# Three groups of TensorE transposes read their tiles as fp32r instead of fp32

## The chip, the cores and the metric

One core of one Trainium2 chip. The metric is the device time of one execution in microseconds (us). TensorE appears in the profile as PE (matmuls) and PEld (weight loads), VectorE as DVE, ScalarE as ACT, GpSimd as POOL, and the queue that starts most of the DMAs as SP.

## The reference

One layer with 1024 positions of width 1024: a root-mean-square norm with a scale and shift computed from c, one input projection, 8 stick-breaking heads and 8 forgetting heads of width 64, a gate, an output projection, and a last norm. Cut to what matters here:

```python
h = rmsnorm(x, g_norm) * (1.0 + scale) + shift          # scale, shift, gate from silu(c) @ w_ada + b_ada
z = h @ w_in                                            # q, k, v of both kinds, gate path, forget logits
# stick-breaking heads: a[t,s] = sigmoid(z_ts) * prod_(s<j<t) (1 - sigmoid(z_tj)), s < t
# forgetting heads:     p = softmax(q k^T * scale + cum_q - cum_k), s <= t
o = probabilities @ v                                   # for each head
y = concat([rmsnorm(o_sb, g), rmsnorm(o_fx, g)]) * silu(g_path)
x = x + (1.0 + gate) * (y @ w_out)
return rmsnorm(x, g_final)
```

## The kernel before

All large products take each operand as a sum of two fp32r halves (hi and lo; fp32r is a 4-byte number with fewer mantissa bits) and add three products: hi with hi, lo with hi, hi with lo. The heads are worked in 8 pairs. A pair has 16 units: two heads by eight blocks of 128 queries. Pairs alternate between stick-breaking (even) and forgetting (odd). Unit g has n = g % 8 + 1 blocks of 128 keys.

The order on each engine is written out by hand. For unit g TensorE runs, in this order:

- half of a projection unit (lines 1581, 1582 and 1589: 16 matmuls of 512 columns in two halves), or in the last pair a part of the output product (line 1680);
- at i = 14 and i = 2 of a pair (i = g % 16) the four transposes of half of a pair's v (`transpose_v`, line 1633), 16 such runs;
- the scores of unit g + 2 (lines 1612 and 1613; a bf16 matmul, line 1616, adds the mask);
- for even g the products of probabilities and v of the two units before (line 1668, the moving operand is 256 or 128 columns);
- the transposes of unit g's probabilities (`transpose_probs`, line 1644), one for each 128x128 block, so n of them in a row.

The scores of a stick-breaking unit go through ACT (two sigmoids, lines 909 and 910), DVE (a scan, line 1237) and POOL (a product, line 698) into the tile U, which is a part of `work`. Those of a forgetting unit go through DVE (line 1250), ACT (exp, line 914), DVE (a reciprocal, line 1260) and POOL (line 704). Then TensorE transposes U into one of two PSUM banks, up to four blocks to a bank. ACT copies the bank as pt_hi (line 949) and DVE subtracts this from the bank as pt_lo (line 1298). These two are what line 1668 reads. `next_bank` (line 1623) waits until DVE is done with the item two before.

Before the pairs, the first 512 rows of x are transposed in eight runs of four (`turn_x`, line 1486), each between projection matmuls. TensorE's first work is a product that spreads c over the partitions (line 1723); ACT (line 782) and DVE (line 1136) wait for it.

The tile `work` has 9 rows of 1024 per partition: U is rows 0 and 1, VT (v before its transpose) is row 6, the first four blocks of x are rows 0 to 3. `ident` is a 128x128 fp32 identity that is loaded from memory. In `nc.tensor.transpose(out, in_, identity)` the block is the stationary operand (the one that PEld loads) and the identity is the moving one.

Of the kernel before, what the change touches and what calls it, by code (L numbers as in the profile page):

```python
# [25 lines left out]
def hybrid_trunk_kernel(nc, x, x_t, c, w_ada_t, const_cols, w_blocks, w_f, w_out, g_final, identity, out):  # L26
    fp32 = mybir.dt.float32
    fp32r = mybir.dt.float32r
# [4 lines left out]
    P = 128  # L33
    SEQ, D = x.shape
# [27 lines left out]
    def tgroups(g):  # L62

        n = g % TB + 1
        return [(a, min(a + 4, n)) for a in range(0, n, 4)]
# [103 lines left out]
    with ctx:  # L169
        def sb(name, shape, dt=fp32):  # L170
            return ctx.enter_context(nc.sbuf_tensor(name, shape, dt))

        def sem(name):
            return ctx.enter_context(nc.semaphore(name))
# [16 lines left out]
        def sb_with_early(name, shape, early_shapes):  # L191

            base = (nc.sbuf_base + 31) // 32 * 32
            whole = sb(name, shape, fp32r)
            size = 4
            for n in shape[1:]:
                size *= n
            assert nc.sbuf_base == base + size
            early, at = [], base
            for i, early_shape in enumerate(early_shapes):  # L200
                early.append(nc.alloc_sbuf_tensor_at(f"{name}_early{i}", early_shape, fp32, offset=at))
                at += 4 * int(np.prod(early_shape[1:]))
            assert at <= nc.sbuf_base
            return whole, early

        h_lo = sb("h_lo", [P, DC, SEQ], fp32r)


        stacks, (w_early, ada_early, x_row6, _, x_row7) = sb_with_early(
            "stacks", [P, 2, 2, 3, SEQ], [[P, 2, DC, P], [P, 3, SEQ], [P, SEQ], [P, 4, SEQ], [P, SEQ]])  # L210
        v_stack, (x_late,) = sb_with_early("v_stack", [P, 2, 2, TB, P], [[P, DC, HALF]])

        pt_hi, (squares_junk, root_diag, roots) = sb_with_early("pt_hi", [P, TB, 2 * P],
                                                                [[P, SEQ], [P, HALF], [P, HALF]])
        pt_lo, (x_rows_late,) = sb_with_early("pt_lo", [P, TB, 2 * P], [[P, 2, SEQ]])
        work = sb("work", [P, 9, SEQ])
        U = [work[:, 0, :], work[:, 1, :]]
        R = [work[:, 2, :], work[:, 3, :]]
        CUM = [work[:, 4, :], work[:, 5, :]]
        VT = work[:, 6, :]  # L220
# [6 lines left out]
        gate_half = spare[:, 0, :]  # L227
        o_shift = spare[:, 1, :].rearrange("p (s n) -> p s n", s=2)
        ident = sb("ident", [P, P])
        ident_bf = sb("ident_bf", [P, P], bf16)  # L230
        mask_f = sb("mask_f", [P, 2, P])
        mask_bf = sb("mask_bf", [P, 2, P], bf16)
# [57 lines left out]
        s_ones = sem("s_ones")  # L290
# [50 lines left out]
        s_id = sem("s_id")  # L341
# [21 lines left out]
        X_BANK = TRANS[0]  # L363
# [3 lines left out]
        def x_row(t):  # L367

            return (work[:, t, :] if t < 4 else (x_rows_late[:, 0, :], x_rows_late[:, 1, :], x_row6[:], x_row7[:])[t - 4])
# [35 lines left out]
        Z = [G_T, R[0], R[1], VT, CUM[0], G_T, R[0], R[1]]  # L405
        RES = Z[STORED:] + [U[1], O_T, U[0]]
        SQUARES = U[0]

# [209 lines left out]
        def _(pool):  # L618
# [75 lines left out]
            def sb_probs(g):  # L694

                n = (g % TB + 1) * P
                pool.wait_ge(s_scan, SB_UNIT[g])
                nc.gpsimd.tensor_tensor(U[g % 2][:, 0:n - 1], U[g % 2][:, 0:n - 1], R[g % 2][:, 1:n],  # L698
                                        ALU.mult).then_inc(s_prob, 1)

            def fx_probs(g):
                n = (g % TB + 1) * P
                pool.wait_ge(s_inv, FX_UNIT[g])
                nc.gpsimd.tensor_scalar(U[g % 2][:, 0:n], U[g % 2][:, 0:n], row_inv[:, g % 2:g % 2 + 1], 1.0,  # L704
                                        ALU.mult, ALU.mult).then_inc(s_prob, 1)
# [71 lines left out]
        def _(act):  # L777
# [121 lines left out]
            def scores_out(g):  # L899
                for j, (a, e) in enumerate(pieces(g)):  # L900
                    if is_sb(g):
# [6 lines left out]
                        bank = SCORE[(S_PIECE[g, j] - 1) % 3][:, 0:e - a]  # L908
                        nc.scalar.activation(U[g % 2][:, a:e], bank, ACT.Sigmoid)
                        nc.scalar.activation(R[g % 2][:, a:e], bank, ACT.Sigmoid, scale=-1.0).then_inc(s_sig, 1)  # L910
                if not is_sb(g):
                    n = (g % TB + 1) * P
                    act.wait_ge(s_max, FX_UNIT[g])
                    nc.scalar.activation(U[g % 2][:, 0:n], U[g % 2][:, 0:n], ACT.Exp, bias=neg_max[:, g % 2:g % 2 + 1],  # L914
                                         accum_out=row_sum[:, g % 2:g % 2 + 1]).then_inc(s_exp, 1)
# [175 lines left out]
        def _(dve):  # L1091
# [37 lines left out]
            nc.vector.memset(ones_square[:], 1.0).then_inc(s_ones, 1)  # L1129
            nc.vector.memset(ss_o, 0.0).then_inc(s_ones, 1)  # L1130
            dve.wait_ge(s_id, 16)
            nc.vector.tensor_copy(ident_bf[:], ident[:]).then_inc(s_maskb, 1)
            dve.wait_ge(s_mask, 3)
            nc.vector.tensor_copy(mask_bf[:], mask_f[:]).then_inc(s_maskb, 1)
# [338 lines left out]

        @block.tensor
        def _(pe):
            pe.wait_ge(s_id, 16)

            def turn_x(n):

                d = first_pieces[n][1]  # L1480
                pe.wait_ge(s_xna, 1 + (d >= 2) + (d >= 4))
                pe.wait_ge(s_xnd, 1 + (d >= 2) + (d >= 4))
                if n >= 1:
                    pe.wait_ge(s_hfull, n)
                for t in range(4):
                    last = nc.tensor.transpose(X_BANK[:, t * P:(t + 1) * P],
                                               x_row(t)[:, d * P:(d + 1) * P], ident[:])
                last.then_inc(s_xt, 1)

            def spread_roots():  # L1490
# [38 lines left out]
            def first_piece(n):  # L1529
# [26 lines left out]
                if n + 1 < DC:  # L1556
                    turn_x(n + 1)
# [62 lines left out]
            def next_bank(item):  # L1620
                n = T_ITEM[item]
                if n > 2:
                    pe.wait_ge(s_tfree, n - 2)
                return TRANS[(n - 1) % 2]

            def transpose_v(p, j):

                pe.wait_ge(s_phi, unit_no[p, "v", j] + 1)
                if (p, j) == (0, 0):
                    pe.wait_ge(s_plo, LO_UNITS[-1, "f", 1])  # L1630
                bank = next_bank(("V", p, j))
                for k in range(4):
                    last = nc.tensor.transpose(bank[:, k * P:(k + 1) * P],
                                               VT[:, (4 * j + k) * P:(4 * j + k + 1) * P], ident[:])
                last.then_inc(s_t, 1)

            def transpose_probs(g):
                pe.wait_ge(s_prob, g + 1)
                if g == 0:
                    pe.wait_ge(s_hfull, DC)  # L1640
                for j, (a, e) in enumerate(tgroups(g)):
                    bank = next_bank(("T", g, j))
                    for k in range(a, e):
                        last = nc.tensor.transpose(bank[:, (k - a) * P:(k - a + 1) * P],  # L1644
                                                   U[g % 2][:, k * P:(k + 1) * P], ident[:])
                    last.then_inc(s_t, 1)

            def sum_squares(p):
# [73 lines left out]
            for half in range(NHALF):  # L1722
                last = nc.tensor.matmul(psum[:, half, :], ones_square[0:1, :], CUM[0][0:1, half * HALF:(half + 1) * HALF],
                                        start=True, stop=True)
            last.then_inc(s_call, 1)
            turn_x(0)
            for n in range(2 * DC):
                if n == 2 * DC - 2:
# [80 lines left out]
```

## Time and profile before

| | |
|---|---|
| time, median of 3 runs | 741.24 us (740.69 to 743.7) |
| the profiled execution | 742.23 us, of which its span is 740.4 us |
| PE busy | 703.8 us, 95% |
| PEld busy | 587.7 us, 79% |
| DVE, ACT, POOL busy | 482.9, 426.0, 370.6 us |
| chain that ended last | PE 80%, DVE 9%, ACT 6% |
| mean granted TensorE clock | 0.988 |

A matmul's row lasts from its start to its modelled end, and rows of PE overlap: the next one starts while the last drains. So how long a matmul holds the engine is read from the distance between starts and not from its duration. A merged row (x8) lasts from the first start to the last end; that length less one duration, over the number less one, is the distance.

### The profile page before, as it was taken

Reading aid. Unit: us, or ns where it says so; the run is one execution under the profiler, and the core shown is the slowest. Engines: PE = TensorE matmul, PEld = TensorE weight load, DVE = VectorE, ACT = ScalarE, POOL = GpSimd, SP = SyncE. Lnnn points to the kernel's source line nnn. Section 1 sums busy time; section 2 is a strip of 40 time slices with the busy share of each in tenths; the row PEclk is TensorE's granted clock in tenths of the full one; section 3 lists DMA queues with packets and bytes.
Section 4 is the critical chain, followed back from the end, with each engine's and each line's share of the span. In section 5 each row is a group of like instructions: output and inputs, shape, how many; then the busy total and the mean of one; then the engine's idle time right before and its main releaser. Section 6 shows DMA issues by size and latency. Waiting matters only on the chain.

```text
span 740.4 us, 10802 instructions
## 1 busy us (share of the span) xinstructions
PE 703.8 (95%) x3830; PEld 587.7 (79%) x3830; DVE 482.9 (65%) x992; ACT 426.0 (58%) x885; POOL 370.6 (50%) x329
## 2 busy tenths in 40 slices
PE   2989988999999999999999999999999999999995
PEld 0667877888888888888888888888888878888884
DVE  4977998646655776465558664765586654555566
ACT  5875767555675656466757565666565665323222
POOL 1020465567885455688756555866575643321100
PEclk9999999999999999999999999999999997999998
DMA  9942231223442110334430102455312095882222
GB/s 350 409 155 86 74 126 32 86 100 114 143 147 102 38 58 0 100 114 153 161 103 12 58 23 87 145 172 168 102 45 79 22 361 165 255 284 86 86 114 114
DMA packets 35463, 93.14 MB, mean 126 GB/s; under 512 B 4297, under 2 KB 5961, under 8 KB 34898
## 3 DMA queue, kind: packets, MB, share of 16 engines
q1 hardware_dynamic: 28450, 73.71, 28.8%
q0 software_dynamic: 5376, 14.68, 6.2%
q10 hardware_dynamic: 1584, 4.05, 1.4%
q8 instruction: 31, 0.51, 0.3%
q14 instruction: 22, 0.18, 0.1%
HBM read 68.81 MB, written 23.63 MB: 125 GB/s over the span
## 4 chain that ended last, share of the span: by engine, by line
PE 80%; DVE 9%; ACT 6%; issue 3%; POOL 1%; DMA 0%; DVEq 0%; ACTq 0%; POOLq 0%
PE psum L1680 12%; PE psum L1581 12%; PE psum L1582 12%; PE psum L1589 12%; PE psum L1668 8%; PE psum L1644 8%; PE psum L1613 4%; PE psum L1612 4%; DVE stacks L1205 2%; DVE work L1237 2%; PE psum L1511 1%; PE psum L1616 1%; ACT work L910 1%; DVE pt_lo L1298 1%; ACT pt_hi L949 1%
## 5 line engine op out<-in xcount | busy, mean ns | idle before, releaser
L1581 PE MATMUL psum<-h_hi,w_hi 128*128 128x512 f32 x448 | 186.2, 416 | 1.9 <-DVE stacks L1205 1.9
L1582 PE MATMUL psum<-h_lo,w_hi 128*128 128x512 f32 x448 | 176.6, 394 | 0.0
L698 POOL TENSOR_TENSOR work<-work 128x127 f32<-128x127 f32 (+3 forms) x64 | 82.9, 1295 | 155.4 <-DVE work L1237 155.4
L949 ACT ACTIVATE pt_hi<-psum 128x512 fp32r<-128x512 f32 (+1 forms) x192 | 87.7, 490 | 103.4 <-PE psum L1644 100.3
L1298 DVE TENSOR_TENSOR pt_lo<-psum,pt_hi 128x512 fp32r<-128x512 f32 (+1 forms) x192 | 100.9, 552 | 59.6 <-ACT pt_hi L949 57.3
L1237 DVE TENSOR_TENSOR_SCAN work<-work 128x128 f32<-128x128 f32 (+3 forms) x64 | 96.2, 1504 | 38.7 <-ACT work L910 38.4
L1589 PE MATMUL psum<-h_hi,w_lo 128*128 128x512 f32 x448 | 120.2, 390 | 0.0
L1581 PEld LDWEIGHTS psum<-h_hi,w_hi 128*128 128x128 f32 x448 | 85.2, 190 | 17.4 <-issue 2.7
L1589 PEld LDWEIGHTS psum<-h_hi,w_lo 128*128 128x128 f32 x448 | 84.2, 188 | 18.6
L1582 PEld LDWEIGHTS psum<-h_lo,w_hi 128*128 128x128 f32 x448 | 85.1, 190 | 14.9
L704 POOL TENSOR_SCALAR work<-work,small 128x128 f32<-128x128 f32 (+3 forms) x64 | 47.8, 747 | 92.4 <-DVE small L1260 92.2
L1644 PE MATMUL psum<-ident,work 128*128 128x128 f32 x576 | 87.8, 279 | 2.4 <-DVE pt_lo L1298 1.5
L914 ACT ACTIVATE work<-work,small 128x128 f32<-128x128 f32 (+3 forms) x64 | 49.8, 778 | 61.3 <-DVE small L1255 61.0
L1668 PE MATMUL psum<-pt_hi,v_stack 128*128 128x256 f32 x320 | 80.4, 286 | 2.0 <-DVE pt_lo L1298 2.0
L1668 PE MATMUL psum<-pt_lo,v_stack 128*128 128x256 f32 x320 | 75.0, 281 | 0.0
L923 ACT ACTIVATE spare<-psum 64x256 f32<-64x256 f32 x64 | 24.3, 380 | 77.6 <-PE psum L1668 77.2
L1612 PE MATMUL psum<-stacks 128*128 128x512 f32 (+1 forms) x192 | 65.7, 342 | 1.9 <-DVE small L1250 1.9
L1644 PEld LDWEIGHTS psum<-ident,work 128*128 128x128 f32 x576 | 62.2, 142 | 4.5 <-issue 1.6
L1613 PE MATMUL psum<-stacks 128*128 128x512 f32 (+1 forms) x192 | 63.6, 344 | 0.0
L1668 PEld LDWEIGHTS psum<-pt_hi,v_stack 128*128 128x128 f32 x320 | 61.3, 192 | 2.2 <-DVE pt_lo L1298 2.2
L1668 PEld LDWEIGHTS psum<-pt_lo,v_stack 128*128 128x128 f32 x320 | 61.0, 191 | 0.1
L1269 DVE TENSOR_TENSOR work<-psum,spare 64x256 f32<-64x256 f32 x64 | 26.7, 416 | 51.0 <-ACT spare L923 50.7
(186 smaller groups left out, 1349.5 us busy)
## 6 DMA issues: line engine op xcount, KB each, us to landing
w_raw<-in_w_blocks SPq DMA_DIRECT2D x30, 512.0 KB, 4.3
w_split_scratch<-work SPq DMA_DIRECT2D x16, 512.0 KB, 3.3
work<-in_x SPq DMA_DIRECT2D x12, 512.0 KB, 7.7
work<-in_w_ada_t SPq DMA_DIRECT2D x10, 512.0 KB, 7.7
y_split_scratch<-work SPq DMA_DIRECT2D x10, 512.0 KB, 3.3
v_stack_early<-in_w_ada_t SPq DMA_DIRECT2D x8, 512.0 KB, 3.2
work<-forget_scratch SPq DMA_DIRECT2D x8, 512.0 KB, 5.3
work<-in_w_out SPq DMA_DIRECT2D x16, 256.0 KB, 3.4
```

What stands on the lines that cost most here:

```text
L698: nc.gpsimd.tensor_tensor(U[g % 2][:, 0:n - 1], U[g % 2][:, 0:n - 1], R[g % 2][:, 1:n], ALU.mult).then_inc(s_prob, 1)
L949: nc.scalar.activation(pt_hi[:, a:e, (g % 2) * P:(g % 2 + 1) * P], bank, ACT.Copy).then_inc(s_thi, 1)
L1237: nc.vector.tensor_tensor_scan(R[g % 2][:, 0:n][:, ::-1], R[g % 2][:, 0:n][:, ::-1], R[g % 2][:, 0:n][:, ::-1], 1.0, ALU.mult, ALU.bypass) ...
L1298: nc.vector.tensor_tensor(pt_lo[:, a:e, q0:q0 + P], bank, pt_hi[:, a:e, q0:q0 + P].bitcast(fp32), ALU.subtract).then_inc(s_tfree, 1)
L1581: nc.tensor.matmul(bank, hi, h_hi[:, c_, cols], start=(c_ == 0), stop=False)
L1582: nc.tensor.matmul(bank, hi, h_lo[:, c_, cols], start=False, stop=False)
L1589: last = nc.tensor.matmul(bank, lo, h_hi[:, c_, cols], start=False, stop=(c_ == DC - 1))
L1612: nc.tensor.matmul(bank[:, 0:c1 - c0], q, stacks[:, p % 2, a, 1, c0:c1], start=True, stop=False)
L1613: last = nc.tensor.matmul(bank[:, 0:c1 - c0], q, stacks[:, p % 2, a, 2, c0:c1], start=False, stop=not diagonal)
L1644: last = nc.tensor.transpose(bank[:, (k - a) * P:(k - a + 1) * P], U[g % 2][:, k * P:(k + 1) * P], ident[:])
L1668: last = nc.tensor.matmul(OUT[:, c0:2 * P], v_stack[:, p % 2, a, k, :], src[:, k, c0:2 * P], start=(k == 0 and n == 0), stop=(k == qb + 1 ...
L1680: last = nc.tensor.matmul(psum[:, bank, :], y_, w_[:, m, cols], start=(j == 0 and k == 0), stop=(j == PAIRS // 2 - 1 and k == 2))
```

## The change

It gives the memory of `work` a second name, `turned`, of type fp32r, makes an fp32r copy of the identity on DVE, and transposes probabilities, v and x with both operands and the output named as fp32r. It is the same memory, the same words, the same instructions in the same order. TensorE's first wait, for the load of the identity, becomes a wait for the copy.

```diff
--- before.py
+++ after.py
@@ -213,7 +213,10 @@
         pt_hi, (squares_junk, root_diag, roots) = sb_with_early("pt_hi", [P, TB, 2 * P],
                                                                 [[P, SEQ], [P, HALF], [P, HALF]])
         pt_lo, (x_rows_late,) = sb_with_early("pt_lo", [P, TB, 2 * P], [[P, 2, SEQ]])
+        work_at = (nc.sbuf_base + 31) // 32 * 32
         work = sb("work", [P, 9, SEQ])
+
+        turned = nc.alloc_sbuf_tensor_at("turned", [P, 9, SEQ], fp32r, offset=work_at)
         U = [work[:, 0, :], work[:, 1, :]]
         R = [work[:, 2, :], work[:, 3, :]]
         CUM = [work[:, 4, :], work[:, 5, :]]
@@ -227,6 +230,7 @@
         gate_half = spare[:, 0, :]
         o_shift = spare[:, 1, :].rearrange("p (s n) -> p s n", s=2)
         ident = sb("ident", [P, P])
+        ident_r = sb("ident_r", [P, P], fp32r)
         ident_bf = sb("ident_bf", [P, P], bf16)
         mask_f = sb("mask_f", [P, 2, P])
         mask_bf = sb("mask_bf", [P, 2, P], bf16)
@@ -1129,6 +1133,7 @@
             nc.vector.memset(ones_square[:], 1.0).then_inc(s_ones, 1)
             nc.vector.memset(ss_o, 0.0).then_inc(s_ones, 1)
             dve.wait_ge(s_id, 16)
+            nc.vector.tensor_copy(ident_r[:], ident[:]).then_inc(s_ones, 1)
             nc.vector.tensor_copy(ident_bf[:], ident[:]).then_inc(s_maskb, 1)
             dve.wait_ge(s_mask, 3)
             nc.vector.tensor_copy(mask_bf[:], mask_f[:]).then_inc(s_maskb, 1)
@@ -1473,7 +1478,7 @@
 
         @block.tensor
         def _(pe):
-            pe.wait_ge(s_id, 16)
+            pe.wait_ge(s_ones, 3)
 
             def turn_x(n):
 
@@ -1483,8 +1488,8 @@
                 if n >= 1:
                     pe.wait_ge(s_hfull, n)
                 for t in range(4):
-                    last = nc.tensor.transpose(X_BANK[:, t * P:(t + 1) * P],
-                                               x_row(t)[:, d * P:(d + 1) * P], ident[:])
+                    last = nc.tensor.transpose(X_BANK[:, t * P:(t + 1) * P].bitcast(fp32r),
+                                               turned[:, t, d * P:(d + 1) * P], ident_r[:])
                 last.then_inc(s_xt, 1)
 
             def spread_roots():
@@ -1630,8 +1635,8 @@
                     pe.wait_ge(s_plo, LO_UNITS[-1, "f", 1])
                 bank = next_bank(("V", p, j))
                 for k in range(4):
-                    last = nc.tensor.transpose(bank[:, k * P:(k + 1) * P],
-                                               VT[:, (4 * j + k) * P:(4 * j + k + 1) * P], ident[:])
+                    last = nc.tensor.transpose(bank[:, k * P:(k + 1) * P].bitcast(fp32r),
+                                               turned[:, 6, (4 * j + k) * P:(4 * j + k + 1) * P], ident_r[:])
                 last.then_inc(s_t, 1)
 
             def transpose_probs(g):
@@ -1641,8 +1646,8 @@
                 for j, (a, e) in enumerate(tgroups(g)):
                     bank = next_bank(("T", g, j))
                     for k in range(a, e):
-                        last = nc.tensor.transpose(bank[:, (k - a) * P:(k - a + 1) * P],
-                                                   U[g % 2][:, k * P:(k + 1) * P], ident[:])
+                        last = nc.tensor.transpose(bank[:, (k - a) * P:(k - a + 1) * P].bitcast(fp32r),
+                                                   turned[:, g % 2, k * P:(k + 1) * P], ident_r[:])
                     last.then_inc(s_t, 1)
 
             def sum_squares(p):
```

## Rows read from the trace of the kernel before

**Rows 1.** The page: busy us, share of the span, instructions of each engine.
```profile
PE 703.8 (95%) x3830; PEld 587.7 (79%) x3830; DVE 482.9 (65%) x992; ACT 426.0 (58%) x885; POOL 370.6 (50%) x329
```

**Rows 2.** Waits of PE, 135 to 600 us: total, times, longest, all in us.
```profile
PE psum L1633 <- ACT work L886: 1.7, 4, 0.4
PE psum L1581 <- DVE stacks L1205: 1.0, 3, 0.5
PE psum L1644 <- DVE v_stack L1277: 0.6, 3, 0.2
```

**Rows 3.** Groups by line and form, PE matmuls: count, busy us, mean ns.
```profile
L1644 PE MATMUL psum<-ident,work 128*128 128x128 f32 x576 | 87.8, 279 | 2.4 <-DVE pt_lo L1298 1.5 <-DVE v_stack L1277 0.6 <-POOL work L698 0.2
L1668 PE MATMUL psum<-pt_hi,v_stack 128*128 128x128 f32 x64 | 14.3, 223 | 0.0
```

**Rows 4.** The same view, weight loads.
```profile
L1644 PEld LDWEIGHTS psum<-ident,work 128*128 128x128 f32 x576 | 62.2, 142 | 4.5 <-issue 1.6 <-DVE v_stack L1277 1.3 <-POOL work L698 1.2
L1668 PEld LDWEIGHTS psum<-pt_hi,v_stack 128*128 128x128 f32 x320 | 61.3, 192 | 2.2 <-DVE pt_lo L1298 2.2
L1653 PEld LDWEIGHTS psum<-ones,work 128*128 128x128 f32 x16 | 1.9, 191 | 0.2 <-POOL work L773 0.2
```

**Rows 5.** Timeline at 306.6 us, unit 49: start, length, engine, line.
```profile
306.65 0.20 PEld L1644 LDWEIGHTS psum<-ident,work 128*128 128x128 f32 x2
306.70 0.39 PE L1644 MATMUL psum<-ident,work 128*128 128x128 f32 x2
...
306.82 0.19 PEld L1581 LDWEIGHTS psum<-h_hi,w_hi 128*128 128x128 f32 x1
...
306.85 0.48 PE L1581 MATMUL psum<-h_hi,w_hi 128*128 128x512 f32 x1
```

**Rows 6.** Timeline, a run of eight transposes in unit 55.
```profile
333.42 1.04 PE L1644 MATMUL psum<-ident,work 128*128 128x128 f32 x8
```

**Rows 7.** Timeline: fp32 matmuls of 512 columns, then loads before one-column fp32 matmuls.
```profile
47.34 1.02 PE L1494 MATMUL psum<-pt_hi_early,ones 128*128 128x512 f32 x2
...
694.70 1.86 PEld L1653 LDWEIGHTS psum<-ones,work 128*128 128x128 f32 x16 [0.19 <-POOL work L773]
```

**Rows 8.** Timeline, four places where TensorE waits for others.
```profile
220.19 0.55 PE L1644 MATMUL psum<-ident,work 128*128 128x128 f32 x3 [0.21 <-DVE v_stack L1277]
...
261.10 0.47 PE L1581 MATMUL psum<-h_hi,w_hi 128*128 128x512 f32 x1 [0.31 <-DVE stacks L1205]
...
291.00 0.66 PE L1633 MATMUL psum<-ident,work 128*128 128x128 f32 x4 [0.43 <-ACT work L886]
...
297.27 0.86 PEld L1644 LDWEIGHTS psum<-ident,work 128*128 128x128 f32 x8 [0.17 <-POOL work L698]
```

**Rows 9.** Chain that ended last, three of its pieces: start, us, what.
```profile
114.62 7.16 issue
...
253.79 0.50 ACT work L910
...
696.64 35.55 PE psum L1680 x156
```

**Rows 10.** Timeline: the first DVE copy and TensorE's first matmul.
```profile
2.69 0.23 DVE L1132 CAST ident_bf<-ident 128x128 bf16<-128x128 f32 x1 [1.66 <-DMA ident<-in_identity]
...
2.71 1.22 PE L1723 MATMUL psum<-work,ones 1*128 1x512 f32 x1 [2.71 <-DMA ident<-in_identity]
```

**Rows 11.** Timeline at 125 us: a wait, and matmuls after it.
```profile
124.98 0.39 PE L1668 MATMUL psum<-pt_hi,v_stack 128*128 128x256 f32 x1 [2.03 <-DVE pt_lo L1298]
...
128.15 0.63 PE L1582 MATMUL psum<-h_lo,w_hi 128*128 128x512 f32 x1
128.58 0.63 PE L1581 MATMUL psum<-h_hi,w_hi 128*128 128x512 f32 x1
```

**Rows 12.** Timeline: POOL's product of unit 35 and the transposes' loads behind it.
```profile
240.03 1.10 POOL L698 TENSOR_TENSOR work<-work 128x511 f32<-128x511 f32 x1
...
241.44 0.42 PEld L1644 LDWEIGHTS psum<-ident,work 128*128 128x128 f32 x4
```

## The prediction

> **What bounds the kernel now.** I read the page first: PE is busy for 703.8 of 740.4 us, while no other compute engine reaches two thirds [rows 1]; by its part on the chain, PE holds 80% of what ended last. A PE row overstates the engine's time, so I went on to what PE waits for. Between 135 and 600 us all its idle time is some 3 us [rows 2]. So in the loop over the pairs TensorE's own stream is the clock, and a nanosecond taken out of it counts, unless the next wait takes it back. The chain by time shows three exceptions, where it runs over ACT, DVE and POOL: the second half of x's projections, units 6 to 10 (with 7.16 us that the profile doesn't explain [rows 9]), and units 113 to 115 with table loads on ACT.
>
> **How long a transpose holds TensorE.** Eight in a row last 1.04 us [rows 6]; less the 0.273 us that one lasts, over 7, that is 0.109 us from start to start. What is it made of? Two things could set it. *The moving side:* a plain fp32 matmul of 512 columns starts 0.43 us after the last (1.02 less 0.59) [rows 7], 0.83 ns a column, so 128 columns would take 0.107 us. Fp32r matmuls of 512 columns take 0.23 us each (156 in 35.55 us) [rows 9], half of it, and an fp32r matmul of 128 columns lasts 223 ns, where the transpose lasts 279 [rows 3]: 56 ns more, which is one more pass of 128 columns. *The load:* the two loads of unit 49 last 0.20 us together, one alone 0.142, so the second started 0.06 us after the first, and the first matmul started 0.05 us after its load [rows 5]. The load of a transposed block is thus through in about 0.06 us and lies beside a stream of 0.107. All other 4-byte loads, fp32 (line 1653) and fp32r (line 1668), last 191 ns against 142 [rows 4], and loads with almost nothing between them follow each other after 0.111 us (1.86 less 0.19, over 15) [rows 7]. So for a plain load the name fp32 or fp32r makes no difference, and being a transpose makes it 50 ns shorter.
>
> **The change, part by part.**
>
> 1. *Transposes.* As fp32r the identity should stream in one pass, 0.056 us. Then the load of the next block is what is late: 0.06 us. No row shows an fp32r transpose. The bounds: 0.056 us if the load hides after all, 0.111 us if the load becomes that of an ordinary fp32r weight. I take 0.065, near the load step of rows 5 and a little above it, because the step was read at 10 ns. That is 0.044 us less for each.
>
> 2. *The last transpose of each run gains nothing.* The matmul behind it needs an ordinary load. In unit 49 line 1581 is loaded at 306.82, its row begins at 306.85 but lasts 0.48 instead of 0.39, so it really streams from about 306.93, 0.11 us after its load began [rows 5]. That load may begin only when the last transpose has begun, so 0.11 us pass in either kernel. Runs: 128 of probabilities, 16 of v, 8 of x. Transposes: 576 [rows 3], 64 and 32, by the loops. Steps that gain: 448 + 48 + 24 = 520. At 0.044 us: 22.9 us.
>
> 3. *What the waits take back.* Where TensorE arrives early at a wait, what was saved since the start of that wait's chain is lost. There is one of each kind in [rows 8].
>    - Line 1581 waits for DVE in unit 40, at 261.10. Its chain left TensorE before ACT's row at 253.79 [rows 9], and units 38 and 39 lie in between, 6 + 7 steps, 0.57 us. It recurs in three pairs: 1.7 us.
>    - v's transposes wait for ACT (291.00, four times). The chain starts at the first bank of unit 45, three steps: 0.5 us in all.
>    - Unit 47 waits for POOL (297.27, four times). In between are the transposes of v and of unit 46, 3 + 6 steps, 0.4 us each: 1.6 us.
>    - The second bank of units 14, 30, 46 and so on waits for v_stack (220.19, seven times, slight in four). Three steps: 0.9 us.
>    - Off the chain: units 6 to 10, 16 steps, 0.7 us; the last run of x, and units 113 to 115 with v: 9 steps, 0.4 us.
>    Sum 5.8 us. Elsewhere POOL is done with the probabilities well before TensorE wants them. One of the closest covers is unit 35's: POOL ends at 241.13 and the transposes' first load begins at 241.44 [rows 12], 0.31 us later, and between its scores and there lie 1 + 3 + 2 steps, 0.26 us. So hardly anything new becomes late. If that cover were gone, all 22.9 us would be lost and not more.
>
> 4. *The copy of the identity.* It stands on DVE ahead of ident_bf. The cast there takes 0.23 us, and TensorE's first matmul, which starts with the identity's landing at 2.71 [rows 10], now waits for the copy. ACT and DVE wait for that product, and their chain leads to the first transpose of x. It costs 0.25 us; below, nothing, if the loads of x turn out to be later. ident_bf and the mask copies behind it have 65 us of room.
>
> 5. *The second name* costs no instruction. What ACT, DVE and POOL do has the same words and forms as before.
>
> Sum: 22.9 - 5.8 - 0.25 = 16.8 us. The profiled execution took 742.23 us, so it would take 725.4. The median of the runs shown is 1.0 us below it, 741.24, which makes 724.4; I say 725.0.
>
> **Two rules beside the rows.** The rows say that a transposed block's load is through in 0.06 us [rows 5]. The Trainium skill (TensorE: Matmul & The Clock Gate, LDWEIGHTS) gives a load as the number of columns over 1.2, that is 107 ns for 128, at any type without fast loading. By that rule the load alone would keep the step where it is and the change would bring nothing. The trace agrees with it for plain loads and not for those of transposes. The Trainium skill (same page, Terms) calls the transpose mode four times faster for fp32. The trace shows a factor of two in the stream (0.107 us against two passes of 0.107 for a plain fp32 product), which leaves one more factor of two for the type; if the fp32 transposes had all four already, nothing would be left.
>
> **The rivals.**
>
> - *A: as worked out.* 718 to 732 us. The low end has a step of 0.056: 520 x 0.053 = 27.6, less 4 for waits, 718. The high end has a load that is only partly hidden, a step of 0.083, half way between 0.056 and 0.111: 520 x 0.026 = 13.5, less 3.5, 732. Chance 0.74.
> - *B: the step does not fall.* Either a transpose named fp32r is loaded as ordinary weights are, every 0.111 us, or a 4-byte word goes through the array in two passes whatever its name. For it: the 191 ns of all fp32r loads [rows 4]. Against it: fp32 and fp32r loads are alike there, so the type is not what makes the transposes' loads short. 520 x 0.002 = 1.0 us, and the copy: 741 to 743 us. Chance 0.19. This is also the case in which the change doesn't do what it says.
> - *C: slower, by the clock.* After the wait of 2.03 us at 124.98 the granted clock fell to half (1.2 GHz) and 512 columns took 0.43 us instead of 0.23 from 126 to 129 us [rows 11]; that cost 1.8 us. If the waits of step 3, each longer by up to 0.6 us, made the clock fall too, 18 of them would cost 32 us less the 16.8 saved: 757 us. Slower by more than 3.7 us begins at 12 such falls. Against it: the waits of [rows 8] are 0.2 to 0.43 us long and the clock stayed at full speed, and with 0.6 more they are still half of that 2.03. Chance 0.06. The Trainium skill (TensorE: Matmul & The Clock Gate, PE-mode transpose) has it that transposes do not count as work for the clock; here eight in a row run at full speed [rows 6]. By that rule shorter transposes would, if anything, help.
> - Faster than 718: 0.01.
>
> **How the numbers follow.** The likeliest is A. A's own range leaves out 0.26, so the range reaches up over B: 718 to 742.5. A measurement of this kernel can tell about 0.5% from no change, 3.7 us. Faster than 737.5: A, 0.75. Within: B, 0.19. Slower than 745: C, 0.06.
>
> **What would show it.** A right: the matmuls of lines 1644, 1633 and 1486 last some 55 ns less, 220 to 225 instead of 273 to 279; their loads still last about 142; eight in a row last 0.65 to 0.72 us instead of 1.04; line 1581 behind them still lasts 0.48; and the idle time between 135 and 600 us [rows 2] grows by 4 to 5 us. If the loads of line 1644 last 190, it is B by the load; if the matmuls still last 273, it is B by the stream. Windows with a low clock where the kernel before has none would be C. The copy is seen by TensorE's first start, 2.95 instead of 2.71. I would be wrong in size if the steps fell as said and the gaps at [rows 8] grew by more than the savings between; then more of the chain hangs on ACT, DVE and POOL than I counted.

## The result, and the profile after

The kernel after takes 738.85 us (median; 737.14 to 740.58), the kernel before 742.45 on the same chips (740.24 to 744.02). The ratio is 0.9949, with an interval of 0.994 to 0.9959. So it is faster by 3.8 us, where 16.8 were forecast: the direction held, the size did not.

The profiled execution of after took 739.11 us, its span is 737.3 and its mean granted clock 0.984, where before had 742.23, 740.4 and 0.988. In after the lines shift by 5: 1644 is 1649, 1633 is 1638, 1486 is 1491, 1581 is 1586, 1668 is 1673, and the ACT, DVE and POOL lines by 4 or 5. The page of after, engines' busy us and shares, against [rows 1]:

```profile
PE 696.8 (95%) x3830; PEld 580.5 (79%) x3830; DVE 483.6 (66%) x993; ACT 425.8 (58%) x885; POOL 371.1 (50%) x329
```

The groups by line and form of after, PE and then loads, against [rows 3, 4]: count, busy us, mean ns, idle time before.

```profile
L1649 PE MATMUL psum<-ident_r,turned 128*128 128x128 f32 x576 | 72.7, 253 | 6.1 <-POOL work L702 2.5 <-DVE pt_lo L1303 1.8 <-DVE v_stack L1282 0.9
...
L1649 PEld LDWEIGHTS psum<-ident_r,turned 128*128 128x128 f32 x576 | 57.4, 142 | 8.3 <-POOL work L702 3.7 <-DVE v_stack L1282 2.5 <-issue 1.9
```

The load's row is unchanged at 142 ns. The matmul's fell from 279 to 253 and not to 220, so the load that looks the same no longer keeps up. The distance shows it. Timeline of after, unit 49 and then the run of eight of unit 55, against [rows 5, 6]: start, length.

```profile
307.00 0.23 PEld L1649 LDWEIGHTS psum<-ident_r,turned 128*128 128x128 f32 x2
307.18 0.19 PEld L1586 LDWEIGHTS psum<-h_hi,w_hi 128*128 128x128 f32 x1
...
333.33 0.86 PE L1649 MATMUL psum<-ident_r,turned 128*128 128x128 f32 x8
334.02 0.46 PE L1586 MATMUL psum<-h_hi,w_hi 128*128 128x512 f32 x1
```

Eight in a row last 0.86 us: less one duration of 0.25, over 7, that is 0.087 us a step. The loads of unit 49 say the same (0.23 less 0.142), where [rows 5] had 0.06. Read singly, in before each load begins 2 ns after the transpose ahead of it and the next transpose 107 ns later: the stream was the limit. In after the loads follow each other every 83 to 88 ns, and a transpose starts some 36 ns after its load. It is so throughout: in the runs of two and more blocks the second load begins 62 ns after the first in before and 86 in after (medians of the 112 runs of probabilities).

Waits of PE from 135 to 600 us in after, against [rows 2]: total, times, longest.

```profile
PE psum L1586 <- DVE stacks L1210: 2.0, 3, 0.9
PE psum L1638 <- ACT work L890: 1.6, 4, 0.4
PE psum L1649 <- DVE v_stack L1282: 0.9, 3, 0.4
PE psum L1649 <- POOL work L702: 0.3, 1, 0.3
```

They grew by 1.5 us in all. At two of the places of [rows 8], timeline of after:

```profile
221.18 0.45 PE L1649 MATMUL psum<-ident_r,turned 128*128 128x128 f32 x3 [0.39 <-DVE v_stack L1282]
...
261.70 0.47 PE L1586 MATMUL psum<-h_hi,w_hi 128*128 128x512 f32 x1 [0.72 <-DVE stacks L1210]
```

Both came later than in [rows 8] (220.19 and 261.10), though TensorE had saved time on the way. Something had been lost earlier. Timeline of after between 108 and 133 us, all the places where PE waits:

```profile
108.02 0.91 PE L1649 MATMUL psum<-ident_r,turned 128*128 128x128 f32 x8 [1.75 <-DVE pt_lo L1303]
109.91 0.77 PE L1586 MATMUL psum<-h_hi,w_hi 128*128 128x512 f32 x1 [0.99 <-DVE stacks L1210]
...
131.66 0.54 PE L1649 MATMUL psum<-ident_r,turned 128*128 128x128 f32 x4 [2.29 <-POOL work L702]
```

From the second on, and again behind the third, the granted clock is at half. The view by windows (us in the window, busy us and instructions of each engine, then PEclk), first of before and then of after:

```profile
108.00:112.00 4.00, 2.51 (x14) 2.09 (x15) 3.92 (x7) 2.66 (x6) 3.31 (x3) 1.00 0.57 183
125.00:129.00 4.00, 4.00 (x14) 3.32 (x15) 3.94 (x5) 2.19 (x6) 3.92 (x4) 0.58 0.17 9
133.00:137.00 4.00, 4.00 (x27) 3.49 (x26) 2.75 (x4) 1.98 (x7) 1.03 (x1) 1.00 0.39 61
```

```profile
108.00:112.00 4.00, 3.00 (x13) 2.51 (x14) 3.89 (x8) 3.39 (x8) 2.93 (x3) 0.61 0.74 246
125.00:129.00 4.00, 4.00 (x23) 3.41 (x23) 3.73 (x5) 2.19 (x6) 3.92 (x3) 1.00 0.17 9
133.00:137.00 4.00, 4.00 (x12) 3.09 (x12) 2.96 (x3) 1.85 (x5) 0.77 (x1) 0.60 0.57 102
```

The last column but two is the clock. Before has one fall here, behind the wait at 124.98 [rows 11]; after has two, at 109 and 133. In the last window after gets through 12 matmuls where before gets through 27; part of that is another mix, since before has come to the short ones of unit 12 there. Like for like, a projection product takes 0.43 us at half clock and 0.23 at full. How far ahead or behind after is, by the start of a unit's transposes (worked out from the trace, after less before):

```
unit   start in before   after   again (experiment 1)
  6        103.20        -0.84        -0.70
 12        136.34        +1.93        -0.69
 48        303.27        +0.34        -2.26
114        604.39        -2.58        -4.83
127        683.47        -3.16        -3.89
```

The profiled execution of after loses 2.8 us between units 6 and 12. From 12 to 114 it gains 4.5 us.

### The profile page after: what moved, and what is told of

The parts are those of the page before. It is cut to its first block, busy times and chain, and to the rows that moved or that the text cites. A ratio compares the mean times of both kernels' runs of the same rounds, so it can differ in the third digit from the quotient of the medians.

```text
span 737.3 us, 10803 instructions
## 1 busy us (share of the span) xinstructions
PE 696.8 (95%) x3830; PEld 580.5 (79%) x3830; DVE 483.6 (66%) x993; ACT 425.8 (58%) x885; POOL 371.1 (50%) x329
## 4 chain that ended last, share of the span: by engine, by line
PE 63%; DVE 13%; ACT 9%; POOL 7%; issue 7%; DMA 0%; DVEq 0%; ACTq 0%; POOLq 0%
PE psum L1685 11%; PE psum L1586 11%; PE psum L1587 10%; PE psum L1594 10%; PE psum L1673 7%; PE psum L1649 4%; POOL work L702 3%; PE psum L1618 3%; PE psum L1617 3%; DVE work L1242 3%; POOL w_lo L648 2%; DVE stacks L1210 2%; DVE work L1255 2%; DVE pt_lo L1303 1%; ACT work L918 1%
## 5 line engine op out<-in xcount | busy, mean ns | idle before, releaser
L1594 PE MATMUL psum<-h_hi,w_lo 128*128 128x512 f32 x448 | 121.9, 394 | 0.0
L1649 PE MATMUL psum<-ident_r,turned 128*128 128x128 f32 x576 | 72.7, 253 | 6.1 <-POOL work L702 2.5
L1649 PEld LDWEIGHTS psum<-ident_r,turned 128*128 128x128 f32 x576 | 57.4, 142 | 8.3 <-POOL work L702 3.7
```

What stands on the lines that cost most here:

```text
L1594: last = nc.tensor.matmul(bank, lo, h_hi[:, c_, cols], start=False, stop=(c_ == DC - 1))
```

## The theories

Three things can have made 3.8 of 16.8, and the experiments are to size each. The step: a transposed block is loaded more slowly when it is named fp32r, although its row looks the same, so a step saves 0.022 us and not 0.044. The waits: they take back more than the quarter that I counted. The clock: falls that before doesn't have, or has where they are hidden. The main rivals are that the limit in the step is not the load (but the matmul itself, a write, or a fixed 86 ns for each fp32r instruction), and that the clock's falls follow the waits and not anything else.

## Experiments

**1. The same kernel again.** Nothing is edited.

> The changed kernel itself, once more, as the yardstick beside the three others on the same chip. Theory (a run of n transposes costs 308 + 109 n ns in fp32 and about 345 + 86 n ns in fp32r; two falls of the TensorE clock between 105 and 140 us cost what was gained there): 0.995 of the kernel before, mean granted clock 0.983 to 0.988, and the executions with the higher clock are the shorter ones. Rival (the saving is the same in every execution, and the clock has no part in it): no relation of clock and time.

739.15 us (738.32 to 739.46), ratio 0.996 (0.9948 to 0.9972). Its profiled execution had a mean clock of 0.986 and none of the falls at 109 and 133. It had the one of before instead. Its timeline, PE:

```profile
110.06 0.47 PE L1586 MATMUL psum<-h_hi,w_hi 128*128 128x512 f32 x1 [0.99 <-DVE stacks L1210]
110.36 0.40 PE L1587 MATMUL psum<-h_lo,w_hi 128*128 128x512 f32 x1
...
124.36 0.39 PE L1673 MATMUL psum<-pt_hi,v_stack 128*128 128x256 f32 x1 [1.86 <-DVE pt_lo L1303]
...
126.21 0.63 PE L1587 MATMUL psum<-h_lo,w_hi 128*128 128x512 f32 x1
```

The same two waits stand ahead of 110.06, and the clock stayed. It lost nothing to unit 12 and was 4.8 us ahead at unit 114 (table above). So the falls at 109 and 133 belong to an execution and not to the kernel. In its five executions the one with the highest clock is the shortest (738.32 at 0.986) and those at 0.983 and 0.984 take 739.15 to 739.46, as expected. But this execution met another: behind a wait of 1.73 us it ran the last pair's products at half clock from 606.8 us on, some 4 us earlier than in after, and its lead fell from 4.8 to 2.9 us at unit 116. All executions with a trace have a fall near there, before's too; from 606 to 630 us the granted clock is 0.79 in before and after and 0.72 here.

**2. fp32r only from pair 1 on.** x, v of pair 0 and units 0 to 15 stay fp32.

```diff
-                    last = nc.tensor.transpose(X_BANK[:, t * P:(t + 1) * P].bitcast(fp32r), ...)
+                    last = nc.tensor.transpose(X_BANK[:, t * P:(t + 1) * P], x_row(t)[:, d * P:(d + 1) * P], ident[:])
...
+                    if p >= 1:
...
+                        if g >= STEPS:
```

> x, v of the first pair and the probabilities of units 0 to 15 are transposed as fp32 again, the rest stays fp32r. Theory (what was gained before unit 12 is given back between 105 and 140 us, by falls of the clock that the kernel before does not have on its critical path): the first 140 us are those of the kernel before, clock 0.988, one fall at about 125 us; the gain behind it is 4.7 us, so about 0.9937 of the kernel before, 1 us faster than the changed kernel. Rival (early transposes gain as the later ones do): the 1.4 us of the early runs are lost, about 0.997 of the kernel before, 1.4 us slower than the changed kernel.

738.65 us (737.18 to 740.58), ratio 0.9956 (0.994 to 0.9972). The time lies between the two expectations and settles nothing: it scatters over 3.4 us, and with the clock (0.989 took 737.18, 0.984 took 739.94 and 740.58). The profile is clearer. Its fall is at 124.8, as in before, and behind it unit 114 begins 4.4 us ahead of before, unit 127 5.0. That is what fp32r in pairs 1 to 7 was worth in this execution, the shortest of the six, in which no fall is added.

**3. The last transpose of each run back to fp32.** 152 transposes: the last of each unit's, of each half of v, and of each four of x.

```diff
+                        if k < g % TB:
                             last = nc.tensor.transpose(bank[:, (k - a) * P:(k - a + 1) * P].bitcast(fp32r),
                                                        turned[:, g % 2, k * P:(k + 1) * P], ident_r[:])
+                        else:
+                            last = nc.tensor.transpose(bank[:, (k - a) * P:(k - a + 1) * P],
+                                                       U[g % 2][:, k * P:(k + 1) * P], ident[:])
```

> The last transpose of each of the 152 runs is fp32 again, all others stay fp32r. Theory (behind a transpose in fp32r the next weight load begins some 20 ns after the transpose's stream has begun, so each run in fp32r costs 19 ns more at its end): runs of 1, 2, 4, 6 and 8 cost 416, 503, 670, 850 and 1010 ns from the start of the matmul before to the second one behind, each 19 less than in the changed kernel; 2.9 us in all, of which the waits leave some 1.8: 0.9925 of the kernel before. Rival (a switch of the type costs as much, or the 19 ns belong to the first transpose of a run): the costs of the runs stay at 435, 522, 688, 869 and 1029 or rise, and the time stays at 0.995 or above.

737.58 us (737.01 to 738.62), ratio 0.994 (0.9928 to 0.9952). That is 1.6 us below experiment 1, where 1.8 were expected from the waits' share, but the two intervals overlap slightly, and the ratio is not the 0.9925 expected; its profiled execution has the falls at 109 and 133 too, with a mean clock of 0.982. The cost of a run can be read from the traces: from the start of the matmul ahead of it (line 1616 in before) to the start of the second matmul behind it. Medians of undisturbed runs, in ns:

```
blocks   before   after   last one fp32
   1       416      435       416
   2       528      523       504
   4       744      688       672
   6       963      869       850
   8      1180     1035      1015
```

(Of the six runs of eight of the last kernel three take 1015 or 1016, the value in the table, and three 1032 to 1035: units 23, 55 and 87, which gain nothing over after. The row of one block is a single run; the others of one block have a different matmul ahead of them and show the same 19 ns, 480 against 499.) Before is 308 + 109n, after 349 + 86n. So fp32r saves 23 ns a step, and each run pays 41 ns once, 18 more than one step gives back; a unit of one block gets slower. With the last one fp32, 16 to 20 ns of that are gone in every row, but for those three runs. What makes the matmul behind an fp32r transpose come later is not shown. Timeline of this kernel, unit 53:

```profile
324.35 0.23 PE L1625 MATMUL psum<-mask_bf,ident_bf 128*128 128x128 bf16 x1
324.39 0.61 PE L1658 MATMUL psum<-ident_r,turned 128*128 128x128 f32 x5
324.83 0.30 PE L1661 MATMUL psum<-ident,work 128*128 128x128 f32 x1
324.89 0.48 PE L1590 MATMUL psum<-h_hi,w_hi 128*128 128x512 f32 x1
325.20 0.40 PE L1591 MATMUL psum<-h_lo,w_hi 128*128 128x512 f32 x1
```

The same unit in after:

```profile
324.54 0.23 PE L1621 MATMUL psum<-mask_bf,ident_bf 128*128 128x128 bf16 x1
324.58 0.69 PE L1649 MATMUL psum<-ident_r,turned 128*128 128x128 f32 x6
325.11 0.46 PE L1586 MATMUL psum<-h_hi,w_hi 128*128 128x512 f32 x1
325.41 0.39 PE L1587 MATMUL psum<-h_lo,w_hi 128*128 128x512 f32 x1
```

From the mask's product to the second projection product it is 0.85 us here and 0.87 in after. The projection's first product starts 0.06 us after an fp32 transpose, and 0.09 after an fp32r one (325.11 less 325.02, where the sixth starts).

**4. Products that keep TensorE at work in its waits.** Units 7 and 11 get 20 products of 512 columns, written to a score bank that is free; the rest is after. They are extra work, and nothing reads them.

```diff
+                for _ in range(count):
+                    nc.tensor.matmul(SCORE[(n - 1) % 3], h_hi[:, 0, 0:P], h_hi[:, 0, 0:HALF], start=True, stop=True)
...
+                if g in {7: 7, 11: 9}:
+                    keep_busy(g, {7: 7, 11: 9}[g])
...
+                if g in {7: 4}:
+                    keep_busy(g, {7: 4}[g])
```

> 20 products that nothing reads fill TensorE's waits in units 7 (7 before and 4 behind its transposes) and 11 (9 before), 512 columns each, into a score bank that is free. Theory (the waits of 1.8 and 2.3 us let the clock fall, and the half clock behind them costs 3.2 and 1.6 us): granted clock 1.00 from 100 to 140 us, unit 12's transposes 2.5 to 3 us earlier, about 736 us, 0.9915 of the kernel before. Rival (DVE and POOL set that stretch, the clock only makes TensorE's own part longer beside them): unit 12's transposes within 0.5 us of where they are now, 0.995.

738.45 us (737.23 to 740.01), ratio 0.9953 (0.994 to 0.9966): no clear gain, a miss. The fall at 109 was gone, but others came. The view by windows of its profiled execution:

```profile
49.00:53.00 4.00, 4.00 (x10) 2.48 (x10) 2.07 (x4) 1.32 (x2) 1.56 (x1) 0.58 0.00 0
127.00:131.00 4.00, 4.00 (x14) 3.14 (x13) 3.94 (x5) 2.17 (x6) 4.00 (x3) 0.57 0.14 9
```

The second stands behind the one long wait that was left open:

```profile
126.26 0.38 PE L1682 MATMUL psum<-pt_hi,v_stack 128*128 128x256 f32 x1 [1.89 <-DVE pt_lo L1303]
```

The first, at 49 us, is behind a wait of 2.08 us at 47.80 that the edit doesn't touch. At unit 6 this execution is 2.1 us behind that of after, but the fall is not all of it: 1.0 us was there before the wait, 0.6 of it from TensorE's first start. The other 1.0 came by the wait itself, which a slower DVE subtraction (1.51 us instead of 0.69) made longer, and the fall together.

**5. The step by itself.** Seven groups of 16 are added at the end, with eight products of 512 columns ahead of each. It ran once (755.44 us), and only its trace is used; the granted clock is 1.00 from 730 to 753 us.

```diff
+            again(lambda c: nc.tensor.transpose(bank[:, c], ident[:], ident[:]))
+            again(lambda c: nc.tensor.transpose(bank[:, c].bitcast(fp32r), ident_r[:], ident_r[:]))
+            again(lambda c: nc.tensor.transpose(bank[:, c.start:c.start + 64], ident[0:64, :], ident[0:64, 0:64]))
...
+            again(lambda c: nc.tensor.transpose(bank[0:64, c], ident[:, 0:64], ident[:]))
...
+            again(lambda c: nc.tensor.matmul(bank[:, c], h_hi[:, 0, 0:P], h_hi[:, 1, 0:P], start=True, stop=True))
```

> The changed kernel with seven groups of 16 transposes or products behind its last product, each after eight products of 512 columns, so the span is longer by the groups themselves. Theory one (a transposed block's load takes its 86 ns in either type, and the fp32 stream of 107 ns hides it): distance from start to start 109 ns for fp32 and 86 for fp32r of 128 by 128; with a stream of only 64 columns behind a load of 128, 86 in both types; with a load of 64 columns and a stream of 128, 109 in fp32 and under 70 in fp32r. Theory two (as fp32 the load takes 62 ns, as fp32r 86): with 64 streamed columns fp32 comes down to 62 and fp32r stays at 86. Theory three (the fp32r stream itself takes 86 ns, a pass and a half): with 64 streamed columns fp32r falls to 45 to 65, and a load of 64 columns leaves it at 86. Plain fp32r products of 128 columns: 111, the load of an ordinary weight.

Timeline of this kernel, PE. The size behind the star is the load's, the next the output's. Line 1788 is fp32r at full size, 1790 and 1792 stream 64 columns (fp32 and fp32r), 1795 and 1797 load 64 (fp32 and fp32r), 1799 is a plain fp32r product:

```profile
731.53 1.91 PE L1786 MATMUL psum<-ident 128*128 128x128 f32 x16
...
735.13 1.50 PE L1788 MATMUL psum<-ident_r 128*128 128x128 f32 x16
...
738.47 1.21 PE L1790 MATMUL psum<-ident 64*128 64x64 f32 x16
...
741.66 1.51 PE L1792 MATMUL psum<-ident_r 64*128 64x64 f32 x16
...
745.06 1.91 PE L1795 MATMUL psum<-ident 128*64 128x128 f32 x16
...
748.64 1.12 PE L1797 MATMUL psum<-ident_r 128*64 128x128 f32 x16
...
751.49 1.90 PE L1799 MATMUL psum<-h_hi 128*128 128x128 f32 x16
```

From start to start, taken singly (medians):

```
load of 128, stream of 128:   fp32 109 ns   fp32r  86 ns   plain fp32r product 111 ns
load of 128, stream of  64:   fp32  63 ns   fp32r  85 ns
load of  64, stream of 128:   fp32 109 ns   fp32r  60 ns
```

Half the stream leaves the fp32r step at 85, half the load brings it to 60. So the fp32r step is the load, 86 ns for 128 columns, and it isn't a fixed price of an fp32r instruction. The fp32 step is the stream, 109; with half of it the load shows, 63 at most. As fp32r the stream is at most 60. The groups with half a stream also load from 64 partitions and not from 128; for full blocks the 62 and 86 ns between the first two loads of a run, in before and after, say the same. Both sides of my sum are thus confirmed for the name under which I read them, and the load is slower under the other. The loads' rows don't tell: 141 ns for line 1788, 139 for line 1790. The Trainium skill (TensorE: Matmul & The Clock Gate, LDWEIGHTS) has one price for a load of 128 columns, 107 ns; the plain one agrees (111), the transposed ones are 86 and at most 63. The Trainium skill (same page, Back-to-back issue gap) has 81 ns for a load and a matmul of 128 columns in a stream of such pairs, which is near the 86 here and not near the 111.

**6. The fills in all the long waits.** 36 products in units 7, 10, 11 and 115, extra work as in experiment 4; the rest is after.

```diff
+                if g == 10:
+                    keep_busy_out(4, 8)
...
+                if g == 115:
+                    keep_busy_out(57, 8)
```

> The changed kernel with products that nothing reads in five waits of TensorE: units 7 (before and behind its transposes), 10 (before the values), 11, and 115 (before the scores), 36 in all. Theory (which of the waits between 105 and 135 us is followed by a fall of the clock differs from execution to execution, and a fall there costs up to 2.6 us in some of them): no low clock between 100 and 140 us and a shorter one at 610 us, executions closer together, 736.5 to 737.5 us, 0.993 of the kernel before. Rival (the stretch is set by DVE and POOL, and the fills only push TensorE back): 738.5 to 739.5, as the changed kernel.

737.0 us (736.02 to 737.91), ratio 0.9928 (0.9909 to 0.9947), with mean clocks of 0.991 to 0.993. By windows:

```profile
108.00:112.00 4.00, 3.93 (x21) 3.02 (x21) 3.89 (x8) 3.22 (x7) 3.14 (x3) 1.00 0.70 213
125.00:129.00 4.00, 4.00 (x22) 3.38 (x22) 3.94 (x5) 2.19 (x6) 3.92 (x4) 1.00 0.17 9
133.00:137.00 4.00, 4.00 (x28) 3.44 (x27) 2.82 (x3) 1.96 (x6) 1.55 (x1) 1.00 0.37 56
```

More work took less time: with no fall between 100 and 600 us the kernel is 5.3 us faster than before and not 3.8. Two things weaken that. The intervals of 0.9928 and of after's 0.9949 overlap slightly. And the fill of unit 115 works on a fall that before has as well: from 606 to 630 us the granted clock is 0.86 here and 0.79 in before, and the lead grows from 4.9 us at unit 114 to 6.1 at unit 116, where in experiment 2 it stayed at 4.4 and 4.3. So up to 1.2 of the 5.3 us are not the change's. The same fills in the kernel before were not run.

There is a second way to take the clock out: to compare executions of equal mean clock. At 0.986 after takes 738.2 us (median of seven, experiment 1 included) and before 743.6 (three, on the chips of the experiments), 5.5 us more; at 0.988 it is 737.14 (one) against 742.1 (eleven), 5.0.

**7. Before, with the last transpose of each unit done twice.** 128 more fp32 steps of 0.109 us, 14.0 us of TensorE.

```diff
+                        if k == g % TB:
+                            last = nc.tensor.transpose(bank[:, (k - a) * P:(k - a + 1) * P],
+                                                       U[g % 2][:, k * P:(k + 1) * P], ident[:])
```

> The kernel before with the last transpose of each of the 128 runs of probabilities made twice, in fp32, so TensorE has 128 x 0.109 = 14.0 us more to do. It asks how much of TensorE's time at this place counts. Theory (some 40% of a change of the runs' cost is taken up by waits): 8 to 9 us slower, 1.012. Rival (TensorE is the bound nearly everywhere and waits take up no more than the 15 to 25% that the prediction counted): 11 to 12 us slower, 1.0155. The 14 us in full would be 1.019.

750.54 us (748.84 to 752.19), ratio 1.0109 (1.0088 to 1.013): 8.1 of the 14.0 us, 58%, as expected. Part of the rest went into waits, which got shorter. These are all of PE from 135 to 600 us in this kernel, 1.6 us where [rows 2] has 3.3:

```profile
PE psum L1633 <- ACT work L886: 1.3, 4, 0.3
PE psum L1644 <- POOL work L704: 0.3, 1, 0.3
```

But not all of the missing 42% is waits. In the profiled executions unit 114 begins 8.5 us later than in before, of 12.4 us added up to there, so waits took 32%. Between units 114 and 116 another 2.4 us came back, and there the clock differs: from 606 to 630 us it is 0.93 here and 0.79 in before. So about a third of a small change to TensorE's transposes is taken up by waits, in this direction too.

**8. All of it together.** Experiment 3 and experiment 6, and TensorE's first product starts on the identity's landing again; only the first transpose of x waits for the copy.

```diff
-            pe.wait_ge(s_ones, 3)
+            pe.wait_ge(s_id, 16)
...
+            pe.wait_ge(s_ones, 3)
             turn_x(0)
```

> The last transpose of each run in fp32, TensorE's first product released by the load of the identity again (only the first transpose waits for the fp32r copy), and the 36 products in five waits. Theory (19 ns for each run, 0.25 us at the start, and the clock's share): 0.2 us earlier at the first transpose of x, 735.5 to 736.5 us, 0.9915. Rival (only the 19 ns hold): 737.5, 0.994.

735.41 us (735.08 to 736.55), ratio 0.9906 (0.9888 to 0.9924), mean clocks 0.991 to 0.993: 7.0 us faster than before and the fastest here, with the fill of unit 115 again a part of it. What the first wait is worth can't be read from its profile, since the identity landed 0.6 us later in this execution (3.32) than in that of before.

## Why the prediction was right in direction and wrong in size

- *What bounds the kernel* held. TensorE's stream is the clock of the pairs, and from 12 to 114 after gained 4.5 us with nothing but transposes changed.
- *Part 1, the step, failed: 0.065 us was 0.087.* The step of it that failed is "near the load step of rows 5". Those rows are of fp32 loads. I had found no difference between plain fp32 and fp32r loads (191 ns both) and carried that to transposed ones, where nothing showed it; and I took the equal length of a load's row for its step. Experiment 5 separates the two. With 23 ns for a step, 520 steps give 12.0 us instead of 22.9. The value lay inside my bounds (0.056 to 0.111) and at the high end of rival A, for which I had 732 us. The measured 738.85 is inside the whole range of 718 to 742.5 only because that was stretched over rival B, whose reason did not hold: that is luck.
- *Part 2, the last of a run, failed in a smaller way.* "0.11 us pass in either kernel" should have been 19 ns more in after (experiment 3), over 152 runs 2.9 us. Together 9.1 to 9.3 us are saved on paper (0.50 us for each eight units, 8.0 in all; v 0.9; x 0.4).
- *Part 3, the waits,* was right in kind and near in size. My 5.8 us were so many steps at 0.044; at 23 ns, and with nothing for the ends of runs, they are 3.0. Measured in the execution of experiment 1: the 28 runs of seven and eight blocks in pairs 0 to 6 should save 3.65 us by the distances of undisturbed runs, and saved 0.33. In and behind them lie the waits for v_stack and those of unit 40's kind, as named. So 3.3 us went there, 36% of 9.3, near the third of experiment 7. The places differ in detail: the waits before line 1586 grew by 1.0 us (I had 1.7, for the full step), those for v_stack by 0.3 on PE and 1.2 on its loads, v's four waits for ACT didn't grow (1.7 and 1.6) where I had 0.5, and those for POOL hardly.
- *Part 4, the copy,* was near. After's first start was 2.96 by this wait, where I had said 2.95; the copy begins at 2.59 there and the first product 0.37 later, where in before it began 0.02 after DVE's first copy [rows 10], so the wait costs 0.35 us and not 0.25. The timeline of after:

```profile
2.59 0.31 DVE L1136 CAST ident_r<-ident 128x128 fp32r<-128x128 f32 x1 [1.57 <-DMA ident<-in_identity]
2.74 0.24 DVE L1137 CAST ident_bf<-ident 128x128 bf16<-128x128 f32 x1
...
2.96 1.22 PE L1728 MATMUL psum<-work,ones 1*128 1x512 f32 x1 [2.96 <-DVE ident_r L1136]
```

- *Part 5, the second name,* cost nothing that shows: ACT, DVE and POOL are busy for as long as before, within 0.7 us.
- *Rival B* fell: the step did. *Rival C* happened in part. I had looked at the short waits [rows 8] and at how often they would lower the clock; they never did. What I didn't look at were the long ones, and where a fall is hidden. The fall of before at 125.7, which I had put at 1.8 us, costs nothing: unit 11's transposes wait for POOL until 131.28. Experiment 6 has no fall there, and they begin no earlier than with one (130.85, and 130.65 in experiment 1). A TensorE that comes earlier waits longer (2.29 us instead of 0.15), and in the profiled execution of after, whose clock was at full speed from 125 to 129, it fell behind that wait, at 133, where nothing hides it. Together with the one at 109 it cost 2.8 us there; the same kernel without the two, in experiment 1, is 2.6 us further at unit 12.
- *The sum again,* with what was measured: 9.3 saved, less 3.3 for the waits, less 0.35 for the copy, is 5.6 us. At equal mean clock 5.0 to 5.5 were measured, and experiment 6 has 5.3, of which up to 1.2 are not the change's. The 1.2 to 1.8 us that are left to the measured 3.8 go with the clock: before has a mean clock of 0.985 to 0.991, most often 0.988, and after between 0.983 and 0.988 over its runs, and within after the time follows it, from 737.14 at 0.988 to 739.4 to 740.6 at 0.983. That added falls cost time is shown by the two executions of one kernel in experiment 1. How often they occur, and so that they make up all of it, is argued from the mean clocks; only two executions of after have a trace, and one of before. Why the clock falls behind one wait in one execution and not in the next is open.

## What to carry to other kernels

Take the price of a transpose, or of any load and matmul pair, from rows of the very type it will have, as the distance from start to start and not as the length of the load's row; where no row shows it, take the middle of the bounds, and count the ends of runs (19 ns a run took a quarter of what the steps saved). Here the waits took back about a third of a change to the step, in either direction. Then ask of each long wait what lies behind it: in one execution a clock that fell behind such waits cost 2.8 us, half of what the change brings, and with 36 extra products in five waits neither of the two executions with a trace (experiments 6 and 8) had a fall between 100 and 600 us.

## What the runs showed of the hardware

- A transposed 128x128 block of 4-byte words takes 86 ns to load as fp32r and at most 63 as fp32, under rows of the same length (141 and 139 ns), and a plain fp32r weight 111 (experiment 5; in before and after 62 and 86 ns between the first two loads of a run). The stream of its 128 columns takes at most 60 as fp32r and 109 as fp32. Each name is fast where the other is slow.
- A run of fp32r transposes costs 16 to 20 ns more than one that ends in an fp32 transpose (experiment 3).
- Waits of 1.7 to 2.3 us lowered the granted clock from 2.4 to 1.2 GHz in some executions and not in others. Behind the same two waits near 108 and 110 us (1.75 and 0.99 us; 1.76 and 0.99) after has a clock of 0.61 from 108 to 112 us, and the same kernel run again 1.00.
